# A decoder step's sample stage with memory attention in rows, and with weights fetched ahead of their stages

## The chip, the cores and the metric

The kernel runs on one core of a Trainium2 chip, as one program. The metric is the device time of one execution in microseconds. TensorE (PE) multiplies matrices, VectorE (DVE), ScalarE (ACT) and GpSimd (POOL) work on elements, and SyncE (SP) does nothing here but issue DMAs.

## The reference

One layer of a hybrid decoder in float32, for a prompt of 1024 tokens and 8 sample sequences of one token each:

```python
h = RMSNorm(x)
q_lat, kv_lat, k_rope, conv_in, q_mem, gate_logits = split(h @ w_in)
y_A = latent_attention(q_lat, kv_lat, k_rope) @ w_o_mla    # 8 heads; samples: 2048 cached tokens in 16 pages
y_B = silu(layer_norm(depthwise_conv31(glu(conv_in)) + b_dw)) @ w_conv_out
y_C = memory_attention(q_mem, k_mem, v_mem) @ w_o_mem      # 4 heads of 128, 256 memory tokens
x = x + (sig(g_a)*y_A + sig(g_b)*y_B + sig(g_c)*y_C) @ w_out
x = x + MoE(RMSNorm(x))                                    # 64 experts, top 8, and a shared one

def memory_attention(q, k, v):                             # per sample: one query for each head
    s = einsum('nlhd,nmhd->nhlm', rms_norm(q), k) * 128 ** -0.5
    return einsum('nhlm,nmhd->nlhd', softmax(s), v)
```

The new rows of the caches and of the convolution's state are outputs as well.

## The kernel before

The program is a row of stages: constants, front, tokens (norms, projections and prompt attention, to about 691 us), sample (to 1161), merge (1162 to 1551), mixer (to 1782) and experts (to 2684). Each stage is a `Core` with its own SBUF tiles and semaphores and one program for each engine; at its end all engines meet at a barrier (L74), and only then does the next stage's first instruction start, its loads among them. `keep` holds the tiles that live across stages: hT (the normed input, transposed), mergedT, oT_s and moT_s (the samples' attention outputs), and arrays in DRAM: fill_dram and late_dram (columns of h @ w_in, computed ahead), o_dram (the prompt's attention outputs).

**Fills.** Some groups of 128 columns of h @ w_in are computed in the tokens and sample stages, between other work of TensorE, and stored in DRAM. A fill is one such group for one third of the tokens (344): 8 matmuls. In the sample stage `late_weights` loads the weights of a group (512 KB) to late_w, fill_w[b % 2], and fill(0) to fill(3) come first on TensorE.

**Sample stage.** A loop over 8 sequences (batches b), and in each over 16 pages of keys n. For each page TensorE computes the keys of the page (L1374, 4 matmuls of 512 columns, which is the bulk of the time), DVE and ACT their norms, and POOL the power -1/2 in four groups (L1109). Work of the batch before stands at fixed n in this loop, on each engine: on TensorE by_key at 4, by_head, share_maximum at 7, contexts at 10, turn_context at 13. The paged attention uses column tiles: the stationary operand has 32 columns, and four such matmuls write to four quarters of the partitions of one bank (scores L1398, contexts L1442). Memory attention doesn't: its scores are 8 products of one column each, mkT[128 x 128] by a query (L1418), which put the keys on partitions; after the shared maximum (by_key, by_head, share_maximum) and exp, the sums of the shares are 2 matmuls with a matrix of ones (L1446) and the outputs are 8 matmuls with one moving column (L1449). Some of these matmuls stand in the trace as two records each: the 8 of L1418 as x16, the 16 of L1442 as x32, the 8 of L1449 as x16, the 2 of L1446 as x4. Semaphores count: s_ready has four increments for a batch.

**Merge.** The units u are 24 column groups times three token groups g, for each of three branches (order: latent attention, memory, conv). A unit is gate(b, g) (8 matmuls of gate weights by hT, L1750), ACT's sigmoid of it (L1650), out(b, g, branch) (4 matmuls by oT, L1758), and DVE's product and sum (L1706, L1710, L1712). SP loads the weights of each b to a ring of 4 (branch_w: rows 0 to 3 for the output weights, 4 to 11 for the gate weights). Beside that DVE computes the depthwise convolution: 4 channel groups times 31 taps (L1685) on hist, between the units, `step` taps after each; ones and hist are set by POOL, the first history needs ACT's sigmoid of the raw rows (L1653). After the taps TensorE sums over channels with a matrix of ones (L1764, L1766) for the layer norm, first mean and then variance; ACT takes a Silu for each channel group (L1665), one for each of four units, which alternate with the gates' sigmoid. Before its first unit's out, TensorE transposes tap_rows (L1773) and the state (L1779). oT, the prompt's attention outputs, is loaded from DRAM by `branch_in`, four DMAs of 512 KB in runs of 512 bytes, issued by ACT (L1629): branch_in(0) first of all, branch_in(1) before unit 4. first_b holds the gate weights of the first group of the conv branch, whose three gates (L1806) stand before the sums.

**Mixer.** For each of 9 token tiles t two halves of 512 columns of mergedT @ w_out (L2173), the residual, the norm, the router and the shared expert's first half. w_out, 4 MB, is loaded by SP in two halves when the stage opens.

**Experts.** The shared expert's second half (L2598) is added to x by DVE (L2490), which first waits for the semaphores of the expert adds, `added`; for the first pass POOL lets two tiny primer DMAs increment them. Then row tables (L2451), gathers by POOL (L2371), and for 64 experts gate and up (L2561), down (L2571, L2579), and adds to DRAM by POOL.

## Time and profile before

| | us |
|---|---|
| median of 3 runs | 2686.42 (2684.85 to 2686.94) |
| the profiled execution | 2686.19 |
| its span, first to last instruction | 2684.4 |
| TensorE busy | 2526.3 (94%) |
| DVE busy | 1040.9 (39%) |
| POOL busy | 778.8 (29%) |
| ACT busy | 599.5 (22%) |
| mean granted clock of TensorE | 0.972 |

The profiled execution is one run of the three's kind; the 1.8 us between its time and its span lie before the first and behind the last instruction. A clock of 1.00 is 2.4 GHz, and 0.50 is 1.2 GHz; the numbers between are mixtures of the two over a stretch. Times in the rows are counted from the span's start. A row such as `1353.16 14.04 PE L1806 MATMUL` is a run of like instructions that starts at the first number and takes the second one; what stands in brackets is the time that the engine was idle before it, and what ended that.

### The profile page before, as it was taken

How to read it: one execution, taken by the hardware profiler on the slowest of the kernel's cores; microseconds unless marked ns; L12 is line 12 of the kernel's file. 1: busy time of each engine (PE TensorE's matmuls, PEld its weight loads, DVE VectorE, ACT ScalarE, POOL GpSimd, SP SyncE). 2: the span in 40 equal slices, each digit the busy share in tenths (PEclk: the TensorE clock that was granted, in tenths of full speed). 3: DMA queues.
4: the chain of work that ended last, by engine and by line, in shares of the span. 5: the costliest groups of instructions: out<-in, count | busy, mean ns of one | idle time of the engine just before them, and what ended most of it. 6: DMA issues, size and time to landing. Idle time of an engine off the chain costs nothing. (4 is left out here: it accounts for less than half of the span.)

```text
span 2684.4 us, 35226 instructions
## 1 busy us (share of the span) xinstructions
PE 2526.3 (94%) x12288; PEld 1688.3 (63%) x12288; DVE 1040.9 (39%) x2279; ACT 599.5 (22%) x1175; POOL 778.8 (29%) x582
## 2 busy tenths in 40 slices
PE   6999999999799999989979989889999999999995
PEld 3566666665555555556645645447777777777774
DVE  3233334545243333229964226534233333332221
ACT  2223333333143333210013101100112222211111
POOL 1000000000044344300000005434555666555452
PEclk9999999999899999989989999999999999999998
DMA  8111111010342221062112161038989999999996
GB/s 262 45 42 51 39 35 40 29 37 22 86 118 61 77 76 52 22 191 60 36 48 64 36 211 56 17 123 288 296 279 330 329 325 329 323 337 365 366 364 198
DMA packets 213118, 406.88 MB, mean 152 GB/s; under 512 B 57464, under 2 KB 140718, under 8 KB 196471
## 3 DMA queue, kind: packets, MB, share of 16 engines
q1 hardware_dynamic: 168382, 314.39, 34.1%
q0 software_dynamic: 28704, 74.32, 11.1%
q10 hardware_dynamic: 15856, 15.92, 1.8%
q8 instruction: 100, 1.64, 0.3%
q14 instruction: 76, 0.61, 0.1%
HBM read 343.53 MB, written 72.83 MB: 155 GB/s over the span
## 5 line engine op out<-in xcount | busy, mean ns | idle before, releaser
L2371 POOL DMA_INDIRECT mergedT<-tokens_normed,gather_rows x308 | 312.6, 1015 | 122.0 <-issue 95.2
L2561 PEld LDWEIGHTS pGe<-xT,we_g 128*128 128x128 f32 x2048 | 272.6, 191 | 47.0 <-issue 23.6
L2561 PE MATMUL pGe<-xT,we_g 128*128 128x160 f32 (+2 forms) x2048 | 285.8, 298 | 10.0 <-DVE xT L2472 9.9
L2561 PE MATMUL pUe<-xT,we_u 128*128 128x160 f32 (+2 forms) x2048 | 280.3, 295 | 0.0
L2561 PEld LDWEIGHTS pUe<-xT,we_u 128*128 128x128 f32 x2048 | 273.6, 191 | 0.0
L2472 DVE STREAM_TRANSPOSE xT<-mergedT 128x1280 f32<-128x1280 f32 (+2 forms) x64 | 154.4, 2412 | 264.6 <-DMA mergedT<-tokens_normed,gather_rows 264.5
L1374 PE MATMUL pKs<-ws_uk,cTs 128*128 128x512 f32 x512 | 251.7, 636 | 1.2 <-issue 1.2
L805 PE MATMUL pFill<-hT,fill_w 128*128 128x344 f32 x768 | 239.5, 456 | 7.1 <-ACT fill_out L514 7.0
L1109 POOL TENSOR_TENSOR rk<-ssk,half 128x32 f32<-128x32 f32 x32 | 173.3, 5427 | 233.0 <-DVE ssk L1229 233.0
L2571 PE MATMUL pYe<-we_d,h_e 128*128 128x512 f32 x512 | 230.1, 592 | 0.0
L805 PEld LDWEIGHTS pFill<-hT,fill_w 128*128 128x128 f32 x768 | 141.7, 190 | 83.7 <-issue 21.8
L1286 DVE TENSOR_REDUCE ssk<-sqs 128x8 f32<-128x512 f32 x128 | 87.5, 684 | 256.5 <-ACT sqs L1167 256.1
L2391 POOL DMA_INDIRECT sums<-mergedT,add_rows x64 | 104.3, 1629 | 269.6 <-issue 102.1
L2426 ACT ACTIVATE mergedT<-pYe,wc 128x512 f32<-128x512 f32 x128 | 88.0, 687 | 414.4 <-PE pYe L2571 377.1
L1750 PE MATMUL pGate<-hT,branch_w 128*128 128x344 f32 x528 | 160.4, 458 | 11.0 <-DMA branch_w<-in_w_o_mla 11.0
L1374 PEld LDWEIGHTS pKs<-ws_uk,cTs 128*128 128x128 f32 x512 | 98.5, 203 | 102.9 <-issue 101.4
L1685 DVE SCALAR_TENSOR_TENSOR y_conv<-hist,taps,y_conv 128x1024 f32<-128x1024 f32 x120 | 154.0, 1284 | 3.4
L2571 PEld LDWEIGHTS pYe<-we_d,h_e 128*128 128x128 f32 x512 | 93.6, 190 | 92.3 <-issue 92.3
L1750 PEld LDWEIGHTS pGate<-hT,branch_w 128*128 128x128 f32 x528 | 101.5, 193 | 64.2 <-DMA branch_w<-in_w_o_mla 11.1
L2173 PE MATMUL pXf<-w_out,mergedT 128*128 128x512 f32 (+1 forms) x288 | 128.7, 602 | 10.1 <-DMA w_out<-in_w_out 10.1
L1758 PE MATMUL pBranch<-oT,branch_w 128*128 128x344 f32 x384 | 117.0, 454 | 10.3 <-DVE gated L1710 10.0
L1167 ACT ACTIVATE sqs<-pKs 128x512 f32<-128x512 f32 x128 | 76.2, 596 | 208.4 <-PE pKs L1374 205.9
(415 smaller groups left out, 3078.0 us busy)
## 6 DMA issues: line engine op xcount, KB each, us to landing
we_g<-in_w_e_gate SPq DMA_DIRECT2D x64, 1024.0 KB
we_u<-in_w_e_up SPq DMA_DIRECT2D x64, 1024.0 KB
we_d<-in_w_e_down SPq DMA_DIRECT2D x64, 1024.0 KB
mergedT<-in_cache_latent SPq DMA_DIRECT2D x96, 128.0 KB, 2.1
raw_columns<-fill_out SPq DMA_DIRECT2D x48, 172.0 KB
fill_w<-in_w_in SPq DMA_DIRECT2D x16, 512.0 KB
branch_w<-in_w_in SPq DMA_DIRECT2D x11, 512.0 KB
mergedT<-tokens_normed,gather_rows POOLq DMA_INDIRECT x308
```

Of the source, the lines that this page charges most:

```text
L805: mm = pe.matmul(pG[:, 0:GN], ring[b % 2][:, k, :], keep.hT[:, k, g * GN:(g + 1) * GN], start=k == 0, stop=k == KD - 1)
L1109: pool.tensor_tensor(rk[b % 2][:, :, g, :], ssk[b % 2][:, :, g, :], half[:, :].rearrange("p (j h) -> p j h", h=NHEAD), ALU.pow).then_inc(S ...
L1374: mm = pe.matmul(pK[n % 2][:, :], cT[b % 2][:, k, n * P:(n + 1) * P], w_uk[:, k, :], start=k == 0, stop=k == KL - 1)
L1685: v.scalar_tensor_tensor(y[:, i, 0:SEQ], hist[:, i, j:j + SEQ], taps[:, i, j:j + 1], y[:, i, 0:SEQ], ALU.mult, ALU.add).then_inc(S["tap"], 1)
L1750: pe.matmul(pG[g][:, 0:n], ring[b % W][:, 4 + k, :], keep.hT[:, k, at:at + n], start=k == 0, stop=k == KD - 1)
L1758: mm = pe.matmul(pY[u % 2][:, 0:n], ring[b % W][:, k, :], branch[:, k, at:at + n], start=k == 0, stop=k == 3)
L2173: mm = pe.matmul(pX[p][0:r, half * 512:(half + 1) * 512], keep.mergedT[:, k, cols_of(t)], w_out[:, k, half * 512:(half + 1) * 512], start= ...
L2371: pool.indirect_dma_start(out=xg[v % 2][:, g, :], out_offset=None, in_=quarter, in_offset=bass.IndirectOffsetOnAxis(ap=gi[v % W][:, g:g + ...
L2391: pool.indirect_dma_start(out=keep.acc_dram[:, :], out_offset=bass.IndirectOffsetOnAxis(ap=si[u % W][:, 0:1], axis=0), in_=yb[u % 2][:, 0, ...
L2472: v.transpose(xT[p][:, :, 0:n * GR].rearrange("p c (g i) -> p g c i", g=n), xg[p][:, 0:n, :].rearrange("p g (j c) -> p g c j", c=KD)).then ...
L2561: mm = pe.matmul(dst[p][:, f * CAP:f * CAP + n], w[r][:, k, f * P:(f + 1) * P], xT[p][:, k, 0:n], start=k == 0, stop=k == KD - 1)
L2571: mm = pe.matmul(pY[half][:, :], h[p][:, f, 0:P], wd[r][:, f, half * 512:(half + 1) * 512], start=f == 0, stop=f == 1)
```

## The change

1. **First weights.** `keep.first_w` [128, 8, 128], 512 KB, lives across the tokens, sample and merge stages. In the tokens stage it is one of the two fill buffers; at its fourth unit from the end SP loads the sample stage's first fill weights to it, and waits for them at the end. In the sample stage fill(0) to fill(2) use it with no wait; after the ninth fill SP loads the gate weights of merge's b = 0 to it.
2. **Memory attention in rows.** Keys are transposed head by head; the scores are four matmuls, one a head, with the query spread to 32 columns as stationary operand and 256 keys as moving one, in four column tiles of pS. Maximum, exp with its sum, reciprocal and product work on rows, on DVE and ACT; two transposes bring the shares to keys on partitions (`turn_share`), and 8 matmuls in column tiles of pQ give the outputs (128 columns each), which one matmul with pick brings to columns. The maximum is no longer shared with the pages' by transposes.
3. **Merge.** gate(0, g) uses first_w. SP first loads the taps with b_dw, g_ln and b_ln as three more rows, the state and the first raw rows, and then weights(0, 0), of which only w_o_mla is left. TensorE does gate(0, 0), the transposes of the taps, and the transposes of the state between gate(0, 1) and gate(0, 2). ACT takes the sigmoid of the first raw rows ahead of the loop. DVE forms the first history and does 6 taps ahead of merge(0); then 3 taps in each of the next three units, 5 or 4 up to U_C, and 4 after. `branch_in` is on POOL's queue, (0) after the state's load and (1) after five units. The four Silus are taken together at one unit. The first gate weights of the conv branch go to first_w after three units.
4. **Mixer.** w_out in four loads of 256 columns; t = 0 in pieces of 256 columns.
5. **Experts.** DVE waits for pass_added, which ACT increments at the start and POOL after the last adds of a pass.

```diff
@@ tokens stage
+                    if u == UNITS - 4:
+                        sp.dma_start(keep.first_w[:, :, :], ...[:, :, LATE_COLUMNS[0]:LATE_COLUMNS[0] + P]).then_inc(S["late_in"], 16)
...
@@ sample stage
-        fill_w = [c.sb(f"late_w{r}", [P, KD, P]) for r in range(2)]
+        fill_w = [keep.first_w, c.sb("late_w1", [P, KD, P])]
...
-                late_weights(0)
                 late_weights(1)
...
+                sp.wait_ge(S["fill_psum"], 9)
+                sp.dma_start(keep.first_w[:, :, :], ...[:, :, C_GATE:C_GATE + P]).then_inc(S["next_in"], 16)
+                sp.wait_ge(S["next_in"], 16)
...
+                def memory_exp(b):
+                    act.wait_ge(S["mm_ready"], 2 * b + 2)
+                    if b >= 1:
+                        act.wait_ge(S["mT_psum"], b)
+                    act.activation(m_row[:, :], pS[:, MT:2 * MT], ACT.Exp, scale=SC_MEM, bias=m_bias, accum_out=m_den).then_inc(S["me_ready"], 1)
...
-                    act.activation(mp[:, :, :], ms[:, :, :], ACT.Exp, scale=SC_MEM)
...
+                    v.tensor_reduce(m_max, pS[:, MT:2 * MT], AX.X, ALU.max).then_inc(S["mm_ready"], 1)
+                    v.tensor_scalar(m_bias, m_max, -SC_MEM, None, ALU.mult).then_inc(S["mm_ready"], 1)
...
+                def memory_share(b):
+                    v.wait_ge(S["me_ready"], b + 1)
+                    v.reciprocal(m_rden, m_den).then_inc(S["mn_ready"], 1)
+                    v.wait_ge(S["mn_ready"], 2 * b + 1)
+                    v.tensor_scalar(m_row[:, :], m_row[:, :], m_rden, None, ALU.mult).then_inc(S["mn_ready"], 1)
...
-                    for n in range(MJ * MH):
-                        mm = pe.matmul(pX[:, n:n + 1], mkT[:, n, :], q_mT[:, n % MH, b:b + 1], start=True, stop=True)
+                    for h in range(MH):
+                        mm = pe.matmul(pS[Q * h:Q * h + Q, MT:2 * MT], q_mT[:, h, b:b + 1].broadcast_to([P, Q]), mkT[:, h, :], start=True, stop=True)
...
+                def turn_share(b):
+                    pe.wait_ge(S["mn_ready"], 2 * b + 2)
+                    for n in range(MJ):
+                        mm = pe.transpose(pR[:, MT + n * P:MT + (n + 1) * P], m_row[:, n * P:(n + 1) * P], I[:, :])
+                    mm.then_inc(S["mT_psum"], 1)
...
                     for n in range(MJ):
-                        pe.matmul(pX[:, 320:320 + MH], onesr[:, :], mp[:, n, :], start=n == 0, stop=n == MJ - 1)
-                    for h in range(MH):
-                        for n in range(MJ):
-                            mm = pe.matmul(pX[:, 328 + h:329 + h], mvs[b % 2][:, n, h * P:(h + 1) * P], mp[:, n, h:h + 1], start=n == 0, stop=n == MJ - 1)
+                        for h in range(MH):
+                            mm = pe.matmul(pQ[Q * h:Q * h + Q, 0:MHD], mp[:, n, h:h + 1].broadcast_to([P, Q]), mvs[b % 2][:, n, h * P:(h + 1) * P], start=n == 0, stop=n == MJ - 1)
...
+                    pe.matmul(pX[:, 328:328 + MH], m_ctx[:, :], pick[:, :, 0], start=True, stop=True)
...
@@ merge, GpSimd (branch_in moved from ACT's program)
+                def branch_in(w):
+                    for k in range(4):
+                        pool.dma_start(oT[:, w, k, 0:SEQ].rearrange("p (t n) -> p t n", t=NT),
+                                       keep.o_dram[:, :, w, k * P:(k + 1) * P].rearrange("t p n -> p t n")).then_inc(o_in[w], 16)
...
+                pool.wait_ge(S["state_in"], 16)
+                branch_in(0)
+                pool.wait_ge(S["unit_psum"], 5)
+                branch_in(1)
...
@@ merge, ACT
-                    if U_VAR + 5 <= u < U_VAR + 5 + KC:
-                        i = u - U_VAR - 5
+                    for i in range(KC if u == U_VAR + 4 + KC else 0):
                         act.wait_ge(S["normed"], i + 1)
                         act.activation(convT[:, i, :], y[:, i, :], ACT.Silu, scale=g_ln[:, i:i + 1], bias=b_ln[:, i:i + 1]).then_inc(S["conv_ready"], 1)
...
@@ merge, DVE
-                done = 0
+                done = 6
+                gated_unit(0)
+                conv(0, done)
                 for u in range(U_END):
                     merge(u)
-                    if u < KC:
-                        gated_unit(u)
-                    step = (3 if u == 0 else 5 - u % 2) if u < U_C else 6
+                    if u < KC - 1:
+                        gated_unit(u + 1)
+                    step = (3 if u < KC - 1 else 5 - (u % 5 == 0)) if u < U_C else 4
...
@@ merge, TensorE
-                for g in range(3):
-                    gate(0, g, g + 1)
+                gate(0, 0, 1)
                 pe.wait_ge(S["small_in"], 64)
...
                     mm.then_inc(S["state_psum"], 1)
+                    gate(0, g + 1, g + 2)
...
@@ mixer
+                    n = 512 if t else 256
+                    for at in range(half * 512, (half + 1) * 512, n):
+                        pe.wait_ge(w_out_in[at // 256], 16)
+                        pe.wait_ge(w_out_in[(at + n) // 256 - 1], 16)
...
@@ experts
+                    if u == NE - 1:
+                        pool.wait_ge(added[0], 16 * NE * q + 16 * NE + 16)
+                        pool.wait_ge(added[1], 16 * TAILS * q + 16 * TAILS + 16)
+                        pool.sem_inc(S["pass_added"], 1)
...
-                    v.wait_ge(added[0], 16 * NE * q + 16)
-                    v.wait_ge(added[1], 16 * TAILS * q + 16)
+                    v.wait_ge(S["pass_added"], q + 1)
```

## Rows read from the trace of the kernel before

**Rows 1.** The page's line of busy times (us, share, instructions).

```profile
PE 2526.3 (94%) x12288; PEld 1688.3 (63%) x12288; DVE 1040.9 (39%) x2279; ACT 599.5 (22%) x1175; POOL 778.8 (29%) x582
```

**Rows 2.** Busy times by stretch; then granted clock, DMA share, GB/s.

```profile
741.00:1012.00 271.00, 269.45 (x1199) 146.40 (x1198) 102.31 (x247) 95.52 (x154) 123.81 (x23) 0.93 0.28 80
1012.00:1104.00 92.00, 91.74 (x446) 50.49 (x445) 36.84 (x93) 32.70 (x55) 44.09 (x9) 1.00 0.14 38
1104.00:1160.00 56.00, 54.69 (x291) 36.49 (x288) 5.25 (x22) 6.87 (x15) 5.43 (x1) 0.97 0.11 34
1560.00:1580.00 20.00, 20.00 (x42) 8.80 (x43) 2.07 (x3) 1.15 (x2) 0.56 (x1) 0.90 1.07 367
```

**Rows 3.** Timeline where the sample stage opens: start, us, engine, line.

```profile
694.63 0.26 SPq L1036 DMA_DIRECT2D pages<-in_page_table  x1
...
702.13 12.01 PE L1329 MATMUL pKs<-hT,late_w 128*128 128x344 f32 x32 [11.24 <-DMA late_w<-in_w_in]
```

**Rows 4.** Timeline, TensorE: the first matmul group of three batches.

```profile
774.09 0.66 PE L1389 MATMUL pRs<-ident,krot 128*128 128x128 f32 x4
...
1017.75 0.66 PE L1389 MATMUL pRs<-ident,krot 128*128 128x128 f32 x4
...
1106.67 0.66 PE L1389 MATMUL pRs<-ident,krot 128*128 128x128 f32 x4
```

**Rows 5.** Timeline, TensorE in the sample stage's loop and tail.

```profile
926.52 1.93 PE L1418 MATMUL pXs<-q_mT,mkTs 128*128 128x1 f32 x16
...
928.30 7.09 PE L1374 MATMUL pKs<-ws_uk,cTs 128*128 128x512 f32 x12
...
1089.34 1.95 PE L1442 MATMUL pXs<-mergedT,p_keys 128*32 128x257 f32 x32
...
1091.77 0.61 PE L1446 MATMUL pXs<-mps,onesr 128*128 128x4 f32 x4
...
1094.02 5.40 PE L1374 MATMUL pKs<-ws_uk,cTs 128*128 128x512 f32 x12
...
1146.77 4.87 PE L1329 MATMUL pKs<-hT,late_w 128*128 128x344 f32 x16
```

**Rows 6.** Timeline of the start of merge.

```profile
1162.06 7.06 ACTq L1629 DMA_DIRECT2D oT<-attention_out  x4
...
1169.69 16.67 PE L1750 MATMUL pGate<-hT,branch_w 128*128 128x344 f32 x48 [10.99 <-DMA branch_w<-in_w_o_mla]
...
1190.98 1.28 ACT L1650 ACT_TABLE_LOAD   x1 [1.80 <-PE pBranch L1758]
...
1192.63 1.05 ACT L1653 ACTIVATE y_conv<-y_conv 128x1032 f32<-128x1032 f32 x1
...
1193.71 1.23 DVE L1696 TENSOR_TENSOR hist<-convT,y_conv 128x1024 f32<-128x1024 f32 x1 [0.33 <-ACT y_conv L1653]
```

**Rows 7.** DVE's costliest group by lines, 1193.6 to 1378.

```profile
L1685 DVE SCALAR_TENSOR_TENSOR y_conv<-hist,taps,y_conv 128x1024 f32<-128x1024 f32 x120 | 154.0, 1284 | 3.4
```

**Rows 8.** Timeline, TensorE in merge.

```profile
1353.16 14.04 PE L1806 MATMUL pGate<-hT,first_b_gate 128*128 128x344 f32 x48
1377.71 9.74 PE L1764 MATMUL pM<-y_conv,ones 128*128 128x512 f32 x16 [10.51 <-DVE y_conv L1692]
...
1434.46 2.55 PE L1758 MATMUL pBranch<-oT,branch_w 128*128 128x344 f32 x8 [1.81 <-DVE gated L1710]
```

**Rows 9.** Timeline of the start of the mixer.

```profile
1551.88 0.99 SPq L1913 DMA_DIRECT2D w_out<-in_w_out  x2
...
1559.94 29.70 PE L2173 MATMUL pXf<-w_out,mergedT 128*128 128x512 f32 x64 [10.10 <-DMA w_out<-in_w_out]
```

**Rows 10.** Timeline of the start of the experts.

```profile
1792.82 1.29 DVE L2490 TENSOR_TENSOR mergedT<-pYe,x 128x512 f32<-128x512 f32 x2 [11.03 <-DMA primer<-in_k_kth]
...
1793.56 3.70 PE L2598 MATMUL pYe<-w_sd,shared_hT 128*128 128x512 f32 x8 [2.25 <-DVE mergedT L2490]
```

**Rows 11.** GpSimd's costliest group by lines.

```profile
L2371 POOL DMA_INDIRECT mergedT<-tokens_normed,gather_rows x308 | 312.6, 1015 | 122.0 <-issue 95.2 <-DVE gather_rows L2461 26.8
```

More of the change, by code:

```diff
@@ L359, in stage_tokens @@
         g_qm = c.sb("g_qm", [P, MHD])
-        ring = [c.sb(f"fill_w{r}", [P, KD, P]) for r in range(2)]
+        ring = [keep.first_w, c.sb("fill_w1", [P, KD, P])]
         staged = [c.sb(f"fill_out{r}", [P, GN]) for r in range(2)]
@@ L1884, in stage_mixer @@
         pR, pC = c.ps("pRf"), c.ps("pCf")
-        w_out_in = [c.sem(f"f_w_out_in{half}") for half in range(2)]
+        w_out_in = [c.sem(f"f_w_out_in{part}") for part in range(4)]
         x_in = [c.sem(f"f_x_in{p}") for p in range(2)]
@@ L2170, in project @@
                         pe.wait_ge(S["x2_ready"], t - 1)
[L2171 to L2174 removed]
+                    n = 512 if t else 256
+                    for at in range(half * 512, (half + 1) * 512, n):
+                        pe.wait_ge(w_out_in[at // 256], 16)
+                        pe.wait_ge(w_out_in[(at + n) // 256 - 1], 16)
+                        for k in range(KD):
+                            mm = pe.matmul(pX[p][0:r, at:at + n], keep.mergedT[:, k, cols_of(t)], w_out[:, k, at:at + n], start=k == 0, stop=k == KD - 1)
                     if half:
```

176 lines of the change are left out of this document (94 added, 82 removed).

## The prediction

> **What bounds the kernel now.** I read the page first. TensorE is busy for 2526 of 2684.4 us [rows 1], so outside the experts only two things can be saved: work or idle time of TensorE, and time that it spends at its lower clock. The page's row of granted clocks dips in the second quarter; the table by stretches sizes that [rows 2]: the loop over batches of the sample stage has 0.93 of full clock over its first 271 us, 1.00 over the next 92 and 0.97 over the last 56. TensorE is busy there all the time, so a share lost is time lost: 0.07 x 271 + 0.03 x 56 = 20.7 us.
>
> The timeline then gives each boundary of stages, and what ended TensorE's wait there: the first fill weights (to 702.13, in a stage that opens at 694.63) [rows 3], the first merge weights (to 1169.69) [rows 6], w_out (to 1559.94) [rows 9], the primer DMAs (DVE's add at 1792.82) [rows 10]. In merge I read DVE by groups: 120 of its 124 taps take 1284 ns each and it waits for hardly anything between the first tap and the last [rows 7]. So DVE, not TensorE, sets merge's first half: it begins when the first gates are there (1193.71) [rows 6], and TensorE idles 10.51 us for the last tap [rows 8]. In the experts stage the work is a rigid chain that starts later or earlier as a whole.
>
> **The change part by part.** The profiled execution took 2686.19 us, 0.2 below the median, so I subtract from it.
>
> *1. First fill weights a stage ahead.* The stage opens at about 694.7; TensorE starts at 702.13, released by late_w [rows 3]. With the weights resident only keep.hT is needed, which is long there. Gain 702.13 - 694.7 = 7.4. The cold start is paid either way: 32 matmuls take 12.01, where 16 at full clock take 4.87 [rows 3, 5]. The rest of the prologue (transposes, page loads) follows behind the fill; SP's loads of pages run until about 736 and the loop on them starts later, which could hold part of this back. I take 7.4, range 3 to 8. The extra SP load in the tokens stage is 512 KB behind fills, hidden by that stage's matmuls.
>
> *2. Memory attention of the sample stage in rows.* Removed for each batch: the 8 score matmuls of one column (16 records), 926.52 to 928.30, 1.8 us; the two sums and 8 value matmuls (20 records), 1091.77 to 1094.02, 2.25 us [rows 5]; two small transposes, 0.1 each. Together 4.25. Added: 4 score matmuls over 256 columns and 8 value matmuls over 128, in column tiles. The nearest row is the paged contexts, 16 matmuls of 257 columns (32 records) in 1.95, 0.12 each [rows 5]; throughput alone gives 4 x 0.12 and 8 x 0.06, 0.49 for each group. Filling and leaving a group costs something that this row hides in its length; I put each group at 1.0, two transposes [128x128] at 0.5 and the extra pick matmul at 0.25: 2.75. ACT's exp gets no longer, DVE gets a maximum over 256, a reciprocal, a scaling and two copies, about 1.5 us on an engine that is busy 37 of 92 us here [rows 2], so it costs TensorE only where a wait is near (by_head and the shared maximum wait for DVE); 0.1 for that. Net 1.4 a batch, 11 over eight. From both sides: at throughput alone 2.4, so 19; if the column tiles did not overlap, each group has 1024 columns at 0.45 us for 512 (5.40 for 12) [rows 5], 0.9, and some 0.8 around it: 1.7 and 1.7, which with the other terms is 4.25, no gain.
>
> The Trainium skill, TensorEngine Tiling (Array Packing), Key Properties, says that changing the tiling mode drains TensorE. The new code changes it two more times a batch; no row here prices that alone. By that rule about half of the 1.0 that stands above for each group is drain; without it the sum would be the 2.4 a batch above.
>
> *3. The clock.* The falls come with the groups of one-column matmuls: the 12 matmuls L1374 behind such a group take 7.09 us once, and 5.40 where the clock stayed up [rows 5]. From 774.09 to 1017.75 five batches take 243.66 us, from 1017.75 to 1106.67 two take 88.92, 44.5 each [rows 4]. So a fall is not certain behind each group, but all are there. TensorE moves hardly any columns for 1.8 to 2.3 us. The change removes both groups. I take 17 of the 20.7 us back, since one or two falls may stay; 5 if the new, short groups still do it.
>
> *4. Start of merge.* Gate weights for b=0 are resident, so gate(0,0) starts at about 1162.1. It costs 7.2: 4.87 for a warm one and 12.01 - 9.74 = 2.3 for the cold start [rows 3, 5]. Then taps transposes, state transposes and gate(0,1) until about 1176; ACT copies 480 columns (0.6, an estimate from its 1.05 for 1032), loads its table, 1.28, and takes the first sigmoid, 1.05 [rows 6]: DVE can form its first history at 1179.2 instead of 1193.71 [rows 6], 14.5 sooner. That is what counts, since DVE then runs through its 184 us of work to 1377.7 without a hole [rows 7, 8]. Now six taps stand before merge(0), which wants oT and the first out. The oT loads, 1024 runs of 512 bytes each, move from ACT's queue (7.06 us for four issues [rows 6]) to POOL's, behind the load of the state, at about 1168.5. DVE asks for them after the history (1.2) and six taps (1.28 each), at about 1188.
>
> The conv ends near 1363. TensorE's 14.04 us of gates for the next branch start at 1353.16 [rows 8], when DVE has done the merges before; the new order has 116 of the 124 taps among those merges, not 106, so they end only a little sooner, at about 1352.3, and the gates at 1366.4. So TensorE and no longer DVE is last. The sums, 9.74 us cold [rows 8], take 7.2 warm (16 matmuls of 512 columns at 5.40 / 12 [rows 5]) and 1 for the short ones: they end at 1374.6, or 1377.2 if cold, where they ended at 1388.4. Gain 11, range 9 to 13.5.
>
> *5. The Silu together.* In the tail of the conv branch TensorE waits 1.81 us for a gated unit three times and 0.5 twice, five rows of which one stands [rows 8], and each round has two of ACT's table loads of 1.28 [rows 6]. With the four Silus in one go two loads are left of eight; the waits, 6.5 us in all, go, and so 7 with the small ones. Range 5 to 8.
>
> *6. w_out in quarters.* TensorE starts at 1559.94, 8.1 us after the first issue at 1551.88, when half the tensor, 2 MB, has come [rows 9]. A quarter is 1 MB, at the 367 GB/s of this stretch [rows 2] 2.9 us less; but all loads share the engines and the first projection then waits for the next quarter, since TensorE is done with 1 MB in about 4 us. I take 2, range 1 to 3.5.
>
> *7. No primers at the start of experts.* DVE's add waits for the primers until 1792.82, and TensorE waits 2.25 for that add [rows 10]. TensorE's wait goes whole; the row tables and the first gather stand behind DVE's adds and move with them, until the loads of the slot tables hold them. I take 2.7, range 2 to 3.5; the chain behind is rigid and passes it on.
>
> *8. Nothing gained or lost.* Fewer slow small loads on SP (inside 4), the load of merge's first gates behind the last fills (hidden behind TensorE's last two fills of 4.87), the wait of POOL for the adds at the end (TensorE is done; the end is the last add DMA in both), aliases in SBUF.
>
> Sum: 7.4 + 11 + 17 + 11 + 7 + 2 + 2.7 = 58.1. 2686.2 - 58.1 = 2628.
>
> **Rivals.** *The clock keeps falling.* For it: other groups (transposes, picks, contexts) move little too, and the new value group stands beside them. Against it: no fall begins anywhere but at the one-column groups. Only 0 to 5 of the 17: 2640 to 2645.
>
> *Loads on POOL priced by row.* POOL's gathers of 128 rows take 1.0 us each [rows 11]. If POOL wrote the 1024 runs of an oT load at that price, 8.1 us each, four take 32.5 and land at about 1203. merge(0) would be at 1206 instead of 1188; DVE stands with it. 18 us of the gain go: 2646. The Trainium skill, DMA: Bandwidth & Descriptors, gives a fit of 2.0 us + bytes / 436 GB/s for a load from POOL's queue: by an estimate from it 3.2 us each, landed long before 1188, and nothing is lost.
>
> *The column tiles run one after the other.* Against it: 16 of 257 columns in 1.95 [rows 5] is far below 16 x 0.23. For it: a short group may not get so far. Then the gain of 1.4 a batch goes, 11 us, and a fall or three of the clock with it (1.7 each by 7.09 against 5.40): 2639 to 2645.
>
> *Slower than before.* One mechanism: the oT loads on POOL. Everything in merge waits behind merge(0). At 1.0 us for 128 rows it loses 18; to eat all 58 us the four must take 4 x 8.1 + 40 = 72 us, 18 us each, 2.2 times the gathers' price. At 20 us each: about 2694.
>
> *It does nothing.* The boundaries' waits might be replaced by others in each stage; but the loads removed are seen as the releasers [rows 3, 6, 9, 10], so that asks for several mishaps.
>
> **How the numbers follow.** Forecast 0.58; clock 0.18; POOL by row 0.12; serial tiles 0.07; slower 0.035; no change 0.015. A difference under 0.2% (5.4 us) can't be told from none here. The forecast's own range: its parts' ranges add in part, 2618 to 2640. The likely combinations of the rivals end at 2646 to 2652. At the low end the groups at throughput alone (-8), the clock whole (-3.7) and merge at its best (-2.5) give 2614. Range 2614 to 2652, which leaves out both rivals together and the slower case. Faster 0.94, same 0.025, slower 0.035.
>
> **What would show it.** In the profile after: PE's first matmul of the sample stage within 1 us of its opening; a clock of 0.99 or more over the batches, and 43 us from one batch to the next (now 44.5 at full clock); DVE's first history about 17 us after merge opens, with no gap before merge(0), and oT landed by then; PE's wait for the last tap gone; no alternating table loads in the conv tail; TensorE in the mixer 5 to 7 us after it opens. I'm wrong if batches take over 44 us at full clock, if the clock is still under 0.96 there, or if DVE stands at merge(0).

## The result and the profile after

The changed kernel takes 2621.65 us (median of 4 runs, 2620.61 to 2622.62) against 2686.03 for the kernel before in the same runs: a ratio of 0.9758, with a 95% interval of 0.9742 to 0.9773, 64.4 us. The profiled execution has a span of 2619.3 us, against 2684.4.

I cut both spans at the same events, the openings of the stages and the first matmul of the loop over batches, and take the differences:

| stretch, from the trace | before | after | gain |
|---|---|---|---|
| start to the first L1389 (after: L1419) | 774.09 | 766.86 | 7.2 |
| from there to the opening of merge | 387.97 | 349.21 | 38.8 |
| merge | 389.82 | 373.16 | 16.7 |
| mixer | 230.82 | 228.44 | 2.4 |
| experts | 901.70 | 901.63 | 0.1 |

The lines of the profile after that answer to those of before follow. First the page's line of busy times, where [rows 1] has 2526.3 us for PE:

```profile
PE 2487.0 (95%) x12240; PEld 1665.7 (64%) x12240; DVE 1044.1 (40%) x2287; ACT 594.9 (23%) x1177; POOL 786.2 (30%) x590
```

Next the table by stretches over the batches; its last three columns are granted clock, DMA share and GB/s:

```profile
741.00:1010.00 269.00, 265.62 (x1306) 137.52 (x1307) 117.84 (x288) 108.70 (x179) 140.81 (x26) 0.99 0.32 88
1010.00:1060.00 50.00, 49.69 (x247) 25.66 (x239) 21.08 (x52) 18.70 (x31) 25.88 (x5) 1.00 0.03 11
```

[rows 2] has a clock of 0.93 over the first batches; here it is 0.99, and 1.00 after. The 0.01 is one stretch at the lower level, 782.1 to 785.5, which begins while TensorE waits.

The timeline where the sample stage opens:

```profile
694.71 0.26 SPq L1041 DMA_DIRECT2D pages<-in_page_table  x1
...
694.75 12.16 PE L1358 MATMUL pKs<-hT,first_w 128*128 128x344 f32 x32 [3.78 <-PEq L74]
```

Against [rows 3] TensorE starts with the stage, not 7.5 us later, and the cold start is paid as before (12.16 for 32 matmuls, 12.01 there).

The first matmul group of three batches:

```profile
766.86 0.66 PE L1419 MATMUL pRs<-ident,krot 128*128 128x128 f32 x4
...
981.57 0.66 PE L1419 MATMUL pRs<-ident,krot 128*128 128x128 f32 x4
...
1065.09 0.66 PE L1419 MATMUL pRs<-ident,krot 128*128 128x128 f32 x4
```

Five batches took 243.66 us [rows 4]; from 766.86 to 981.57 they take 214.71. The last two take 83.52, 41.8 each, where two without a fall of the clock took 88.92. Batches of 42 us follow each other now; only the first takes 46.65, with 3.0 us in which TensorE waits for DVE's first scores, and the one fall of the clock.

TensorE around the two new groups of a batch (L1451 scores, L1486 values), one stretch of the timeline for each:

```profile
904.09 0.64 PE L1451 MATMUL pSs<-mkTs,q_mT 128*32 128x256 f32 x8
904.66 5.42 PE L1403 MATMUL pKs<-ws_uk,cTs 128*128 128x512 f32 x12
...
923.37 1.95 PE L1479 MATMUL pXs<-mergedT,p_keys 128*32 128x257 f32 x32
925.25 0.62 PE L1481 MATMUL pXs<-new_b,p_new 1*32 1x257 f32 x2
925.79 0.64 PE L1486 MATMUL pQs<-mvs,mps 128*32 128x128 f32 x16
926.37 5.42 PE L1403 MATMUL pKs<-ws_uk,cTs 128*128 128x512 f32 x12
```

What counts is from start to start: the scores hold TensorE from 904.09 to 904.66, the values from 925.79 to 926.37. [rows 5] has 1.8 and 2.25 us at these places. Behind each group 12 matmuls take 5.42, the warm time.

The start of merge, from the timeline of all engines:

```profile
1116.17 6.59 PE L1795 MATMUL pGate<-hT,first_w 128*128 128x344 f32 x16 [3.52 <-DVEq L1711]
...
1124.13 3.67 POOL L1659 DMA_DIRECT2D oT<-attention_out  x4 [7.38 <-DMA ln_mean<-in_state_conv]
...
1130.19 1.28 ACT L1676 ACT_TABLE_LOAD   x1
...
1132.66 1.23 DVE L1738 TENSOR_TENSOR hist<-convT,y_conv 128x1024 f32<-128x1024 f32 x1 [19.78 <-ACT y_conv L1676]
...
1140.55 0.50 PEld L1803 LDWEIGHTS pBranch<-oT,branch_w 128*128 128x128 f32 x2 [6.90 <-DMA oT<-attention_out]
...
1145.42 0.51 DVE L1748 TENSOR_TENSOR mergedT<-gate_sig,pBranch 128x344 f32<-128x344 f32 x1 [3.91 <-ACT gate_sig L1694]
```

Against [rows 6]: the gate starts 0.1 us after the stage opens (7.6 before), DVE's first history 16.6 us after it (31.7 before). Then comes what is new: TensorE stands 6.35 us for oT, four DMAs that POOL issued from 1124.13 on, and DVE 3.91 us at its first merge. The table by stretches has granted clock, DMA share and GB/s last; the DMA engines are busy throughout while oT comes:

```profile
1124.00:1132.00 8.00, 8.00 (x33) 5.50 (x34) 0.00 (x0) 2.94 (x4) 3.67 (x4) 1.00 1.11 308
1132.00:1140.00 8.00, 2.20 (x8) 1.14 (x6) 7.06 (x7) 0.55 (x1) 0.00 (x0) 0.82 1.03 386
```

Further on in merge, TensorE alone:

```profile
1305.40 4.93 PE L1803 MATMUL pBranch<-oT,branch_w 128*128 128x344 f32 x8 [4.77 <-DVE gated L1752]
1310.12 14.55 PE L1851 MATMUL pGate<-hT,first_w 128*128 128x344 f32 x48
1324.51 7.03 PE L1809 MATMUL pM<-y_conv,ones 128*128 128x512 f32 x16
...
1368.80 21.22 PE L1803 MATMUL pBranch<-oT,branch_w 128*128 128x344 f32 x72 [0.58 <-DVE gated L1752]
```

[rows 8] has a wait of 10.51 for the last tap before a cold 9.74; the sums now follow the gates directly and take 7.03. The wait of 1.81 for each gated unit in the tail is gone: 72 matmuls run without one.

The start of the mixer:

```profile
1489.23 5.40 SPq L1958 DMA_DIRECT2D w_out<-in_w_out  x4
...
1494.63 10.74 PE L2221 MATMUL pXf<-w_out,mergedT 128*128 128x256 f32 x39 [7.45 <-DMA w_out<-in_w_out]
```

TensorE starts 5.4 us after the first issue, not 8.1 [rows 9].

The start of the experts, all engines, and the first gate-and-up matmul:

```profile
1721.18 0.69 DVE L2542 TENSOR_TENSOR mergedT<-pYe,x 128x512 f32<-128x512 f32 x1 [4.46 <-PE pYe L2649]
...
1732.53 1.06 POOL L2418 DMA_INDIRECT mergedT<-tokens_normed,gather_rows  x1 [10.67 <-DVE gather_rows L2513]
...
1747.69 2.93 DVE L2524 STREAM_TRANSPOSE xT<-mergedT 128x1536 f32<-128x1536 f32 x1 [8.64 <-DMA mergedT<-tokens_normed,gather_rows]
...
1751.25 3.76 PE L2649 MATMUL pZe<-w_sd,shared_hT 128*128 128x512 f32 x4 [6.06 <-DVE mergedT L2542]
```

```profile
1760.19 5.47 PE L2612 MATMUL pGe<-xT,we_g 128*128 128x192 f32 x32
```

DVE's first add comes 3.5 us after the stage opens (10.1 before [rows 10]) and the first gather 14.9 after it (17.9 before). But the first gate-and-up matmul, L2612, comes 42.5 us after the opening, as before (42.4). The kernel before has these lines of its timeline there:

```profile
1814.37 2.94 DVE L2472 STREAM_TRANSPOSE xT<-mergedT 128x1536 f32<-128x1536 f32 x1 [5.51 <-DMA mergedT<-tokens_normed,gather_rows]
...
1817.94 1.98 PE L2598 MATMUL pZe<-w_sd,shared_hT 128*128 128x512 f32 x4 [2.94 <-DVE mergedT L2490]
...
1825.10 5.47 PE L2561 MATMUL pGe<-xT,we_g 128*128 128x192 f32 x32
```

Its turn of expert 0 (L2472) started 31.7 us after the opening, this one's (L2524) 30.0: of 3.1 us 1.7 are left. Then TensorE, which had stood 2.94 us behind that turn, stands 6.06 us, and its clock is at 1.2 GHz from 1748.0 to 1754.9: four matmuls take 3.76, not 1.98. They end 37.3 us after the opening, 37.2 before, so that nothing is left of the 1.7.

### The profile page after: what moved, and what is told of

Same layout as the page of the kernel before. It is cut to its first block and busy times, and to the rows that moved or that the text cites. A ratio compares the mean times of both kernels' runs of the same rounds, so it can differ in the third digit from the quotient of the medians.

```text
span 2619.3 us, 35201 instructions
## 1 busy us (share of the span) xinstructions
PE 2487.0 (95%) x12240; PEld 1665.7 (64%) x12240; DVE 1044.1 (40%) x2287; ACT 594.9 (23%) x1177; POOL 786.2 (30%) x590
## 5 line engine op out<-in xcount | busy, mean ns | idle before, releaser
L2612 PEld LDWEIGHTS pGe<-xT,we_g 128*128 128x128 f32 x2048 | 272.7, 191 | 46.6 <-issue 24.2
L2612 PE MATMUL pGe<-xT,we_g 128*128 128x160 f32 (+2 forms) x2048 | 286.0, 298 | 9.1 <-DVE xT L2524 9.0
L2612 PE MATMUL pUe<-xT,we_u 128*128 128x160 f32 (+2 forms) x2048 | 280.3, 295 | 0.0
L2612 PEld LDWEIGHTS pUe<-xT,we_u 128*128 128x128 f32 x2048 | 273.6, 191 | 0.0
L2524 DVE STREAM_TRANSPOSE xT<-mergedT 128x1280 f32<-128x1280 f32 (+2 forms) x64 | 154.3, 2412 | 266.0 <-DMA mergedT<-tokens_normed,gather_rows 266.0
L1403 PE MATMUL pKs<-ws_uk,cTs 128*128 128x512 f32 x512 | 234.4, 600 | 1.2 <-issue 1.2
L1403 PEld LDWEIGHTS pKs<-ws_uk,cTs 128*128 128x128 f32 x512 | 92.5, 191 | 98.1 <-issue 97.1
L1795 PE MATMUL pGate<-hT,branch_w 128*128 128x344 f32 x480 | 143.7, 453 | 0.0
L2221 PE MATMUL pXf<-w_out,mergedT 128*128 128x512 f32 (+2 forms) x320 | 128.9, 560 | 7.5 <-DMA w_out<-in_w_out 7.5
L499 POOL TENSOR_TENSOR r<-n,minus_half 128x16 f32<-128x16 f32 x9 | 26.1, 2899 | 328.5 <-DVE n L685 328.5
L808 PE MATMUL pFill<-hT,fill_w 128*128 128x344 f32 x384 | 119.9, 456 | 4.6 <-ACT fill_out L517 4.5
L808 PE MATMUL pFill<-hT,first_w 128*128 128x344 f32 x384 | 119.6, 457 | 2.5 <-ACT fill_out L517 2.5
L1795 PEld LDWEIGHTS pGate<-hT,branch_w 128*128 128x128 f32 x480 | 91.3, 190 | 47.3
```

Of the source, the lines that this page charges most:

```text
L808: mm = pe.matmul(pG[:, 0:GN], ring[b % 2][:, k, :], keep.hT[:, k, g * GN:(g + 1) * GN], start=k == 0, stop=k == KD - 1)
L1403: mm = pe.matmul(pK[n % 2][:, :], cT[b % 2][:, k, n * P:(n + 1) * P], w_uk[:, k, :], start=k == 0, stop=k == KL - 1)
L1795: pe.matmul(pG[g][:, 0:n], ring[b % W][:, 4 + k, :] if b else keep.first_w[:, k, :], keep.hT[:, k, at:at + n], start=k == 0, stop=k == KD - 1)
L2221: mm = pe.matmul(pX[p][0:r, at:at + n], keep.mergedT[:, k, cols_of(t)], w_out[:, k, at:at + n], start=k == 0, stop=k == KD - 1)
L2524: v.transpose(xT[p][:, :, 0:n * GR].rearrange("p c (g i) -> p g c i", g=n), xg[p][:, 0:n, :].rearrange("p g (j c) -> p g c j", c=KD)).then ...
L2612: mm = pe.matmul(dst[p][:, f * CAP:f * CAP + n], w[r][:, k, f * P:(f + 1) * P], xT[p][:, k, 0:n], start=k == 0, stop=k == KD - 1)
```

## The experiments

Each was timed in alternation with the kernel before. The medians of the kernel before lie between 2684.3 and 2686.7 in these series; the interval of a ratio is about 0.13% to either side, 3.5 us. A difference between a run and the changed kernel has the intervals of both ratios, some 5 us together. Smaller ones are read from the traces of stages, one profiled execution each, and told as such.

**1. Memory attention as before, all else changed.** The sample stage's functions for the memory attention are those of the kernel before, with the first weights resident.

```diff
-                        mm = pe.matmul(pS[Q * h:Q * h + Q, MT:2 * MT], q_mT[:, h, b:b + 1].broadcast_to([P, Q]), mkT[:, h, :], start=True, stop=True)
+                        mm = pe.matmul(pX[:, n:n + 1], mkT[:, n, :], q_mT[:, n % MH, b:b + 1], start=True, stop=True)
... (and by_key to turn_context, scale to finish, exps as before)
```

> The changed kernel with the sample stage's memory attention as it was (keys on partitions, one-column matmuls), all else changed. Theory A (the sample stage gained 38.7 us in two parts: 19.7 of TensorE work, 2.5 a batch, and 19 because the clock no longer falls behind the one-column groups): about 2660 us, batches of 44.5 us where the clock stays up and 48 to 50 where it falls, and a mean clock near 0.93 over the first six batches. Rival B (the clock was restored by something else, such as the earlier start of the fills, and only the work counts): about 2641 us, with the clock at 0.99 in the loop.

2659.67 us, 38.0 over the changed kernel; ratio to before 0.9899 (0.9884 to 0.9915). Its batches take 49.01, 48.04, 48.04, 49.73, 48.01, 44.64 and 44.27 us: those of the kernel before but for the first. The clock falls once at 784, about where the changed kernel has its one fall, and seven more times from 825.0 on, until 999. Over the first batches it is at 0.94:

```profile
741.00:1004.00 263.00, 260.41 (x1176) 142.59 (x1175) 100.30 (x244) 92.36 (x150) 124.44 (x23) 0.94 0.28 80
```

So the whole 38 us belongs to this part, and the clock did not come from the earlier start. B is out.

**2. The one-column matmuls put back beside the new ones.** Their results are not used.

```diff
                     for h in range(MH):
-                        mm = pe.matmul(pS[Q * h:Q * h + Q, MT:2 * MT], ...)
+                        pe.matmul(pS[Q * h:Q * h + Q, MT:2 * MT], ...)
+                    for n in range(MJ * MH):
+                        mm = pe.matmul(pX[:, 400 + n:401 + n], mkT[:, n % MH, (n // MH) * P:(n // MH + 1) * P], q_mT[:, n % MH, b:b + 1], start=True, stop=True)
...
+                    for n in range(MJ):
+                        pe.matmul(pX[:, 416:416 + MH], onesr[:, :], mp[:, n, :], start=n == 0, stop=n == MJ - 1)
+                    for h in range(MH):
+                        for n in range(MJ):
+                            mm = pe.matmul(pX[:, 424 + h:425 + h], mvs[b % 2][:, n, h * P:(h + 1) * P], mp[:, n, h:h + 1], start=n == 0, stop=n == MJ - 1)
```

> The changed kernel with the removed one-column matmuls put back beside the new ones, their results unused: 8 of one column behind the scores, 2 with ones and 8 of one column behind the values. Theory A (the one-column groups themselves bring the clock down): 4.05 us a batch of work, 32 in all, and falls of the clock again, 1.7 us for each, 10 to 20 in all: 2664 to 2674 us. Rival B (the groups only cost their own time): 2654 us, clock at 0.99 or more over the loop. Rival C (the column-tiled groups beside them keep the clock up): as B.

2669.21 us (ratio 0.9941, 0.9926 to 0.9956), 47.6 over the changed kernel. All batches but the first and the last take 47.6 to 47.9 where the changed kernel has 41.9 to 42.2: 4.05 of work and 1.7. The timeline of TensorE at the scores of a batch:

```profile
869.77 0.64 PE L1451 MATMUL pSs<-mkTs,q_mT 128*32 128x256 f32 x8
870.34 2.15 PE L1453 MATMUL pXs<-q_mT,mkTs 128*128 128x1 f32 x16
872.35 6.88 PE L1403 MATMUL pKs<-ws_uk,cTs 128*128 128x512 f32 x12
```

The 16 records of one column hold TensorE for 2.0 us, and the clock falls within them: the twelve matmuls behind take 6.88, not 5.42. It falls once in every batch, and in the changed kernel, which has the same column-tiled groups alone, it fell once in the whole loop. So the one-column groups cause the falls. B and C are out. Not every such group does: here, from the second batch of the loop on, only the one at the scores brings a fall, and in the kernel before the four groups of the two batches from 1017.75 to 1106.67 bring none. What decides that isn't shown.

**3. One more column-tiled group a batch, by itself.**

```diff
                     pe.wait_ge(S["m1_ready"], b + 1)
+                    for h in range(MH):
+                        pe.matmul(pQ[Q * h:Q * h + Q, MT:2 * MT], q_mT[:, h, b:b + 1].broadcast_to([P, Q]), mkT[:, h, :], start=True, stop=True)
                     pe.transpose(pX[0:1, 64:64 + JH], m1[:, :], I[:, :]).then_inc(S["m1T_psum"], 1)
```

> The changed kernel with one more column-tiled group for each batch, four matmuls of 256 columns ahead of by_head's transpose, its results unused; it stands alone between matmuls of full height and width, so it changes the form twice. If throughput alone counts (as the two new groups of the changed kernel show, 0.57 us each): +0.6 a batch, 4.6 in all, 2626 us. If a change of form drains TensorE, as I had put into the 1.0 for a group: +1.0 a batch or more, 8 and up, 2630 us or more.

2625.71 us (ratio 0.9776, 0.9763 to 0.9790), 4.1 over the changed kernel, and the batches take 42.41 where they took 41.92: 0.49 each. TensorE at that place:

```profile
918.61 0.64 PE L1463 MATMUL pQs<-mkTs,q_mT 128*32 128x256 f32 x8 [0.18 <-DVE m L1266]
919.18 0.27 PE L1464 MATMUL pXs<-ident,m 128*1 128x128 f32 x1
```

From 918.61 to 919.18 is 0.57, throughput alone (four at 0.12 from [rows 5]) 0.49, and the batch is longer by just that. So the two changes between full matmuls and column tiles cost no more than 0.08 us together; the 4.1 us in the time are by themselves too little to tell.

**4. oT loads issued at once on GpSimd's queue.**

```diff
-                pool.wait_ge(S["state_in"], 16)
                 branch_in(0)
```

> The changed kernel with the first four oT loads on GpSimd's queue issued when merge opens, not behind the load of the state. In the changed kernel DVE stood 3.9 us at its first merge and TensorE 6.35 for these loads, which were issued 8 us after the stage opened and landed 24 us after it. Theory A (they were late because they were issued late): they land 8 us sooner, the stall of 3.9 goes, about 2618 us. Rival B (they share the DMA engines with 4.5 MB of other loads and are late by that): they land at most 3 us sooner, 2619 to 2621. Rival C (they take bandwidth from the state and the first raw rows): the first history of DVE comes later by 2 us or more, no gain, 2621 or more.

2619.48 us (ratio 0.9756, 0.9742 to 0.9769), 2.2 under the changed kernel and within its interval. The trace shows both effects (timeline of the start of merge; it opens at 1116.34):

```profile
1116.98 3.67 POOL L1659 DMA_DIRECT2D oT<-attention_out  x4
...
1125.77 0.63 PE L1822 MATMUL pM<-ident,ln_mean 120*128 120x120 f32 x4 [2.38 <-DMA ln_mean<-in_state_conv]
...
1134.54 1.23 DVE L1737 TENSOR_TENSOR hist<-convT,y_conv 128x1024 f32<-128x1024 f32 x1 [21.38 <-ACT y_conv L1675]
...
1135.92 4.79 PE L1802 MATMUL pBranch<-oT,branch_w 128*128 128x344 f32 x16
```

oT is there when TensorE wants it, at 1135.92, and DVE has no stall. But the state comes late: TensorE waits 2.38 for it (0.77 in the changed kernel) and the first history comes 18.2 us after the opening, not 16.6. Merge takes 370.6 us against 373.2: 2.6 less, of which 2.3 are the 3.9 of A less the 1.6 of C.

**5. The same, and the raw rows of groups 1 to 3 only when oT has landed.**

```diff
+                sp.wait_ge(o_in[0], 64)
                 for i in range(1, KC):
                     gated_rows(i)
```

> As the run before, and the raw rows of groups 1 to 3 (3 MB) are loaded only when oT has landed. Theory A: no more gain than in the run before, 2618 us. Theory B (bandwidth): oT lands well before DVE asks for it (about 20 us after the stage opens), the stall of 3.9 goes and no new one comes, 2617 to 2618 us, where the run before keeps a stall.

2619.00 us (0.9751, 0.9737 to 0.9764), merge 373.7 in its trace, which is that of the slowest of its five executions (2625.42): TensorE waits 2.93 for the state and the first history comes 20.7 us after the opening. It gives no more than the run before. It says little on bandwidth, because in run 4 the first of these 3 MB were issued only at 1129.68, when the state had landed: they could not hold it up there either. What it does show is how long oT takes. SP, which now waits for it, goes on 17.2 us after the opening, 16.5 us after the first of the four issues. In the changed kernel, which issues them 7.4 us later, it is 16.4. So oT was late there because it was issued late, as A of run 4 had it.

**6. oT loads on ACT's queue, as before the change, but all else changed.**

```diff
+                branch_in(0)
                 act.sem_inc(S["gated"], 1)
                 act.wait_ge(S["taps_psum"], 1)
... (branch_in on ACT, branch_in(1) before unit 4; none on GpSimd)
```

> The changed kernel with the oT loads on ACT's queue, four at once when merge opens (7.1 us of issue, as before the change), and not on GpSimd's. If GpSimd's queue writes such a load about as fast as a hardware queue moves it, this is as the variant that issues them at once on GpSimd's queue: about 2618 us. If GpSimd's 1024 runs for each load are the slow part, this one lands well ahead of it. Its own risk: ACT's copy of the taps waits behind the issues, and the small loads share the engines with 2 MB: the first history may come 1 to 3 us later.

2626.46 us (0.9779, 0.9766 to 0.9793), 4.8 over the changed kernel, and merge takes 377.7, 4.6 more. Its timeline (merge opens at 1116.09):

```profile
1116.10 12.68 ACTq L1667 DMA_DIRECT2D oT<-attention_out  x4
...
1136.18 1.23 DVE L1737 TENSOR_TENSOR hist<-convT,y_conv 128x1024 f32<-128x1024 f32 x1 [23.28 <-ACT y_conv L1672]
...
1145.06 10.06 PE L1802 MATMUL pBranch<-oT,branch_w 128*128 128x344 f32 x24 [7.33 <-DMA oT<-attention_out]
```

The four issues hold ACT for 12.68 us, not the 7.1 expected, so that its copy of the taps comes at 1128.9, and oT lands 29 us after the opening although it was asked for first. GpSimd issues the same four in 3.67. Neither expectation held. In merge's trace the move to GpSimd's queue is worth 4.6 us, of the 16.7 that merge gained. My rival of a price by row is out by the changed kernel's own trace: its 32.5 us would have ended at 1157, and oT was there at 1140.5.

**7. DVE's wait for the primers back.**

```diff
-                    v.wait_ge(S["pass_added"], q + 1)
+                    v.wait_ge(added[0], 16 * NE * q + 16)
+                    v.wait_ge(added[1], 16 * TAILS * q + 16)
... (and pass_added with its increments gone)
```

> The changed kernel with DVE's wait for the primer DMAs at the start of the experts as it was. Theory A (the 3.1 us that the first gather gained were lost again: 1.4 in the landing of the gathers, 1.8 in a fall of TensorE's clock after it stood 6 us behind DVE's turn of the first expert): no difference, 2621 to 2622 us, first gate-and-up matmul 42.4 us after the stage opens, no fall of the clock at about 30 us. Rival B (the step was worth its 2.7 and something else in the stage lost as much): 2624 to 2625 us.

2623.51 us (0.9761, 0.9748 to 0.9774), 1.9 over the changed kernel, not to be told from none. The first gate-and-up comes 44.95 us after the opening, 2.4 later than in the changed kernel's profile, and the clock does fall, twice for 3.4 us, in the stretch before it. Neither theory is settled by it alone.

**8. The experts' part alone, on the kernel before.**

```diff
-                    v.wait_ge(added[0], 16 * NE * q + 16)
-                    v.wait_ge(added[1], 16 * TAILS * q + 16)
+                    v.wait_ge(S["pass_added"], q + 1)
... (pass_added incremented as in the changed kernel)
```

> The kernel before the change with the experts' part alone: DVE waits for pass_added and not for the primer DMAs. Theory A (the first gather comes 1.5 to 3.1 us sooner and all of it is lost behind DVE's turn of expert 0, where TensorE stands about 6 us and its clock falls for 7): as the kernel before, 2684 to 2688 us; first gate-and-up matmul 42.4 to 44.9 us after the stage opens. Rival B (the step alone is worth the 2.4 us by which the changed kernel's first gate-and-up came sooner than with the primers put back): 2682 to 2684 us, 40 us after the opening.

2686.82 us against 2684.48 for the kernel before in the same series: 1.0008 (0.9999 to 1.0017). No gain. The first gather comes 14.8 us after the opening, TensorE then stands 6.2 us behind DVE's turn, its clock falls for 7 us, and gate-and-up comes at 42.6. In the profiles of kernels with pass_added and the adds in the changed kernel's order that time is 42.5, 42.6, 42.9, 44.5, 44.6, 44.6, 44.7, 44.8 and 44.9 us; in the two with primers it is 42.4 and 44.95. The six of 44.5 us and more have one thing that the three others lack: a fall of the clock for 3.4 us within the first 3 us of the stage. The step moves nothing that can be seen, and run 7's 2.4 us is within that spread.

**9. DVE's adds ahead of its turns.**

```diff
-                    for t in range(2, 5):
+                    for t in range(2, 7):
                         add(t)
                     turn(q, 0)
-                    for t in range(5, 7):
-                        add(t)
-                    turn(q, 1)
                     for t in range(7, NTT):
                         add(t)
+                    turn(q, 1)
```

> The changed kernel with DVE's adds for tiles 5 and 6 ahead of its turn of expert 0, and those for 7 and 8 ahead of its turn of expert 1. Theory A (TensorE stood 6 us because its banks were freed only behind the turn, which waited for the gathers): TensorE goes through its shared outputs without a stop, its clock stays up, the first gate-and-up matmul starts about 34 to 36 us after the stage opens, not 42.5: 2614 to 2616 us, if the chain behind is rigid. Rival B (row buffers for tiles 4 to 7 wait for stores, so the stop only moves): gain 0 to 3. Rival C (the experts' later part is bound by the chain of add DMAs, which starts no sooner): 2621.

2613.03 us (0.9729, 0.9715 to 0.9742), 8.6 under the changed kernel. The waits of TensorE between the opening and the first gate-and-up, longest last column, first in the changed kernel and then here:

```profile
PE pZe L2649 <- DVE mergedT L2542: 6.1, 1, 6.1
PE pYe L2649 <- issue: 3.6, 1, 3.6
PE pYe L2649 <- DVE mergedT L2542: 1.5, 1, 1.5
```

```profile
PE pYe L2647 <- issue: 3.6, 1, 3.6
PE pYe L2647 <- DVE mergedT L2542: 1.4, 1, 1.4
PE pGe L2610 <- DVE xT L2524: 1.0, 1, 1.0
```

The wait of 6.1 us for DVE is gone. The clock stays up (1.00 from 1716 to 1752, 0.92 from 1717 to 1761 in the changed kernel). The first gate-and-up comes 35.7 us after the opening, 6.8 sooner, and the stage takes 893.9 us, not 901.6. A holds: DVE's order costs this stage 7.7 us. No run has this order together with the primers.

**10. Runs 4 and 9 together.**

> The two edits that gained, together: oT loads at once on GpSimd's queue (2.6 us less in merge's trace) and DVE's adds ahead of its turns in the experts (7.7 us less in that stage's trace). Theory A (the two are in different stages and add): 10.3 us under the changed kernel, 2611 to 2612 us. Rival B (an earlier end of merge is given back in the experts, where the DMA engines are busy): as the adds alone, 2613 to 2614 us.

2610.33 us, ratio 0.9717 (0.9704 to 0.9730). Its merge takes 373.5 us although the code there is that of run 4. TensorE in its timeline:

```profile
1124.23 0.79 PE L1822 MATMUL pM<-ident,ln_mean 120*128 120x120 f32 x4 [2.97 <-DMA ln_mean<-in_state_conv]
1124.81 6.37 PE L1794 MATMUL pGate<-hT,first_w 128*128 128x344 f32 x16
```

TensorE waits 2.97 us for the state, 0.6 longer than in run 4, and its clock is at 1.2 GHz for 3.4 us from 1124.6 on, so that the 16 gate matmuls take 6.37, not 4.80. DVE's first history comes 20.6 us after the opening; run 5's trace has the same second fall. So the 2.6 us of run 4's trace are not a steady gain. Its interval overlaps that of run 9.

**11. As run 10, the oT loads behind the small rows.**

```diff
-                pool.wait_ge(S["state_in"], 16)
+                pool.wait_ge(S["small_in"], 64)
                 branch_in(0)
```

> As the run before, with the oT loads behind the load of the small rows (taps and three vectors), not at once: issued about 6 us after merge opens. If the state's load, which the earlier oT loads held up by 1.9 us, is then on time (first history 16.6 us after the stage opens, not 18.2) and oT still lands before DVE's first merge, merge takes 369 us, 2609 to 2610 in all. If oT lands after the sixth tap, the stall of the changed kernel is partly back: 371 to 373, 2611 to 2613.

2610.44 us (0.9724, 0.9711 to 0.9737). The first history is on time (16.5 us after the opening), oT comes 4.4 us late for TensorE, DVE stands 2.74, and merge takes 370.8. Between the two ends I expected, in merge nearer to the second; the state was late by 1.6 us in run 4's trace, not by the 1.9 that I wrote. Runs 10 and 11 are the fastest kernels of the study, 74 us or 2.8% under the kernel before; what of them belongs to oT isn't settled.

**12. The Silus one for each unit.**

```diff
-                    for i in range(KC if u == U_VAR + 4 + KC else 0):
+                    for i in range(u - U_VAR - 5, u - U_VAR - 4) if U_VAR + 5 <= u < U_VAR + 5 + KC else ():
```

> The changed kernel with the four Silus taken one for each unit, as before the change. Theory A (the eight table loads of 1.28 us and the units that wait for them cost what the conv tail gained): merge takes 6.7 us longer, 380 us, 2628 us in all. Rival B (a part of that gain came from the other edits of merge): +2 to +4.

2627.96 us (0.9790, 0.9777 to 0.9803), 6.3 over the changed kernel; merge takes 380.1 us, 6.9 more. That is the whole gain of the conv tail. A holds.

## Why the prediction was right or wrong

The range and the sign held, and 2628 was 6 us too high. That is partly luck: by the traces the parts came to 65.1, not 58.1, 10.8 more than forecast in the sample stage's loop and 3.7 less at the start of merge and in the experts. Only the sample stage's memory attention, the Silus, the oT loads and the primers have runs of their own; the other parts are read from the two traces. By its steps:

- **First fill weights: right.** 7.4 forecast, 7.2 in the trace; at most 0.2 of it was held back behind the fills.
- **Memory attention, the work: right mechanism, one term too large.** Forecast 11, measured 19.8 (38.8 less the 19 of the clock; run 1 gives 38.0 for both). The term that was off is "each group at 1.0": the groups hold TensorE for 0.57 and 0.58. The two transposes, put at 0.5, take 0.28, and the pick matmul 0.14, not 0.25. These four terms are 1.57, not 2.75, and 4.25 less 1.57 is 2.7 a batch, which is what batches at full clock show (44.65 before, 41.92 after); over eight 21.5. That the result is so near to the bound that I had called throughput alone, 19, is chance: the first batch gained less, with TensorE's new wait of 3.0 us for the scores. The Trainium skill, TensorEngine Tiling (Array Packing), Key Properties, has a drain at each change of mode; run 3 adds such a group by itself and finds 0.49 a batch, which is throughput, so no price for a change shows here.
- **The clock: right.** 17 forecast, 19 measured: 20.7 lost before, 1.7 after, in one fall. Runs 1 and 2 show the cause: with the one-column groups the falls are there, with the same column-tiled groups alone they are not. Why some one-column groups bring none stays open.
- **Start of merge: right but for the oT loads.** The first history was forecast 17.1 us after the opening and came at 16.6. I had left out only that oT could be late by less than a price for each row: issued at 1124.1, it was there at 1140.5, 16.4 us for 2 MB, beside weights, state and raw rows. DVE stood 3.9 us at merge(0), which I had named as a sign of being wrong, and for this step it was. The gates for the next branch started at 194.0 us after the opening, not 190.2. The sums ended 9.9 us sooner; 11 had been said, near my end for cold sums (11.2). They were warm, for which my own times give 13.8, and the stall took 3.9 of that: two misses that hid each other. The estimate by the fit of the Trainium skill, DMA: Bandwidth & Descriptors, Anatomy of one DMA — SWDGE (gpsimd) path, 3.2 us for each load, would give 12.8 for four, one after the other, 3.6 less than the trace shows. The estimate left out that the engines moved other loads too: 308 and 386 GB/s in the two stretches from 1124 to 1140, some 5.6 MB in all, of which 2 are oT's.
- **The Silu together: right.** 7 forecast, 6.7 in the trace, 6.9 by the trace of run 12.
- **w_out in quarters: right.** 2 forecast, 2.4 in the trace.
- **No primers: wrong.** 2.7 forecast, 0.1 measured, and nothing in run 8. The step that failed is "TensorE's wait goes whole ... the chain behind is rigid and passes it on". The chain was not rigid at its next link. The first gather came 3.1 us sooner, but the turn of expert 0, which waits for gathers to land, only 1.7. DVE's program has that turn ahead of the adds that free TensorE's banks, so DVE reached its wait sooner and stood there longer (8.64 us, 5.51 before); TensorE stood 6.1 us behind it and came out of it at 1.2 GHz, which cost 1.8 more. Run 9 shows that this order is costly: with the adds ahead of the turn 7.7 us are gained in the stage. That just the forecast 2.7 went this way is read from one trace before and one after, and profiles of this stage differ by 2.4 us among themselves.

Of the rivals, the clock that keeps falling and the price by row are out by the trace after, the serial column tiles by the 0.57 and 0.58 of the new groups there (they would have taken 0.9 and more) and by run 3, and the slower or unchanged kernel by the time.

## What to carry to other kernels

A group of matmuls that moves one column each can cost more than its own 2 us: look at the granted clock behind it, and turn the product round so that the long dimension moves. When a wait is removed at the head of a chain, look at the next wait in the program of the same engine, and at who is queued behind that; putting the work that others wait for ahead of it was worth more here than the removal. For a large load at the opening of a stage, reckon with its time from issue to landing beside the others: these 2 MB took 16.4 us issued 8 us after the opening and 16.5 issued at once, where they in turn made the state 1.6 to 2.4 us late (runs 4, 5 and 10). And a queue that belongs to an engine with work to do can hold that engine, ACT for 12.68 us in run 6.

## What the runs showed of the hardware

Four DMA issues of 1024 runs of 512 bytes each held ACT for 7.06 us in the kernel before and for 12.68 us in run 6; why it took longer there isn't known. GpSimd issued the same four in 3.67 us. I had looked for the danger on GpSimd's side. A column-tiled group of four matmuls of 256 columns that stands alone costs 0.49 us a batch, no more than its share of a long series of them. And a TensorE that is busy 269 of 271 us can still lose its clock: in the kernel before nine falls to 1.2 GHz, of 3.4 or 6.8 us, begin there in groups of matmuls of one column or within 1.5 us behind them.
